# Weight-block sums of a Strassen-Winograd FFN made by adding transfers instead of GpSimd instructions

## What is computed

```python
def _swiglu(h, w_gu, w_down):
    g, u = jnp.split(h @ w_gu, 2, axis=-1)
    return (jax.nn.silu(g) * u) @ w_down
# in each layer:
h = h + _swiglu(_rmsnorm(h, norm_ffn[i]), ffn_w_gu[i], ffn_w_down[i])
```

## Time and profile before

| | |
|---|---|
| timed runs | 1211.78, 1214.74, 1216.09 us (median 1214.74) |
| profiled execution | 1215.77 us, span 1213.9 us, mean granted clock 0.988 |
| PE busy | 1133.1 us (93%) |
| DVE busy | 863.2 us (71%) |
| POOL busy | 672.8 us (55%) |
| ACT busy | 537.8 us (44%) |
| DMA | 98.32 MB, mean 81 GB/s; 97.16 MB of it through SyncE's queue, none from GpSimd's |

### The profile page before, as it was taken

How to read it: one execution, slowest core, us unless ns; L and a number is a source line. 1 busy time by engine, 2 the same in 40 slices (tenths; PEclk the granted TensorE clock), 3 DMA queues, 4 the chain that set the end, 5 groups by cost and what they waited for, 6 DMA issues and landing times.

```text
span 1213.9 us, 18428 instructions
## 1 busy us (share of the span) xinstructions
PE 1133.1 (93%) x7114; PEld 1011.2 (83%) x7114; DVE 863.2 (71%) x1260; ACT 537.8 (44%) x1053; POOL 672.8 (55%) x583
## 2 busy tenths in 40 slices
PE   9999998899899998999999999997989899988897
PEld 8877676888788988978998888876988788988786
DVE  6688776688744889845398888675898435889643
ACT  6487634454301545411277777433544103445202
POOL 6477654777424676534255545645776225776442
PEclk9999998999999999999999999998999999999999
DMA  6311133223333332332211001141323332332331
GB/s 189 99 35 53 36 109 82 70 71 104 96 96 88 87 105 70 107 95 93 80 38 38 18 19 35 53 142 49 105 73 91 96 106 77 98 103 72 96 96 70
DMA packets 175397, 98.32 MB, mean 81 GB/s; under 512 B 7880, under 2 KB 171216, under 8 KB 175312
## 3 DMA queue, kind: packets, MB, share of 16 engines
q1 hardware_dynamic: 175296, 97.16, 28.1%
q10 hardware_dynamic: 16, 0.00, 0.0%
HBM read 94.01 MB, written 2.10 MB: 79 GB/s over the span
## 4 chain that ended last, share of the span: by engine, by line
PE 51%; DVE 30%; ACT 7%; issue 7%; POOL 4%; DMA 1%; DVEq 0%; ACTq 0%; POOLq 0%
PE bank L1640 13%; PE bank L1644 13%; PE bank L1643 13%; DVE w_lo L2937 7%; DVE gate_up L2969 5%; DVE f_lo L2974 3%; DVE gate_up L2953 3%; DVE gate_up L2958 3%; ACT w_hi L1292 3%; PE bank L2346 2%; ACT f_hi L1317 2%; DVE gate_up L2954 2%; DVE g_lo L2937 1%; PE bank L2365 1%; PE bank L2368 1%
## 5 line engine op out<-in xcount | busy, mean ns | idle before, releaser
L1640 PE MATMUL bank<-x_hi,w_lo 128*128 128x256 f32 (+1 forms) x424 | 136.8, 323 | 21.4 <-DVE w_lo L2937 12.6
L1640 PE MATMUL bank<-f_hi,w_lo 128*128 128x512 f32 (+1 forms) x363 | 141.6, 390 | 13.5 <-DVE f_lo L2974 13.5
L1643 PE MATMUL bank<-f_lo,w_hi 128*128 128x512 f32 (+1 forms) x363 | 140.3, 387 | 0.0
L1644 PE MATMUL bank<-f_hi,w_hi 128*128 128x512 f32 (+1 forms) x363 | 140.2, 386 | 0.0
L1643 PE MATMUL bank<-x_lo,w_hi 128*128 128x256 f32 (+1 forms) x424 | 134.9, 318 | 0.0
L1644 PE MATMUL bank<-x_hi,w_hi 128*128 128x256 f32 (+1 forms) x424 | 134.8, 318 | 0.0
L835 POOL TENSOR_TENSOR s<-raw 128x512 f32<-128x512 f32 x40 | 64.1, 1601 | 104.0 <-DVE g_lo L2937 74.0
L822 POOL TENSOR_SCALAR w_hi<-raw 128x1408 fp32r<-128x1408 f32 x32 | 44.0, 1376 | 127.6 <-PE bank L1644 116.3
L853 POOL TENSOR_TENSOR gate_s<-gate_s,rs_t 128x512 f32<-128x512 f32 x44 | 65.9, 1497 | 81.5 <-ACT gate_s L1309 81.5
L2937 DVE TENSOR_TENSOR w_lo<-raw,w_hi 128x1024 fp32r<-128x1024 f32 x80 | 93.8, 1173 | 22.7 <-ACT w_hi L1292 22.7
L1640 PEld LDWEIGHTS bank<-x_hi,w_lo 128*128 128x128 f32 x424 | 83.8, 198 | 28.5 <-issue 14.2
(11 more groups left out here) (372 smaller groups left out, 3849.8 us busy)
## 6 DMA issues: line engine op xcount, KB each, us to landing
raw<-in_ffn_w_gu SPq DMA_DIRECT2D x80, 512.0 KB, 5.2
raw<-in_ffn_w_down SPq DMA_DIRECT2D x32, 704.0 KB, 4.6
w_raw<-in_a_w_qkv SPq DMA_DIRECT2D x10, 512.0 KB, 4.7
w_raw<-in_a_w_o SPq DMA_DIRECT2D x8, 512.0 KB, 4.0
w_raw<-in_ffn_w_gu SPq DMA_DIRECT2D x8, 512.0 KB, 3.9
w_raw<-in_b_w_o SPq DMA_DIRECT2D x8, 512.0 KB, 3.8
w_raw<-in_b_w_in SPq DMA_DIRECT2D x4, 672.0 KB, 4.0
w_raw<-in_b_w_uq SPq DMA_DIRECT2D x4, 576.0 KB, 3.9
```

Of the source, the lines that this page charges most:

```text
L1640: first = pe.matmul(o, ll, rh, start=start, stop=False)
L1643: pe.matmul(o, lh, rl, start=False, stop=False)
L1644: return pe.matmul(o, lh, rh, start=False, stop=stop)
```

## The change

GpSimd no longer adds. ScalarE writes the negated a21 and a22 into one of two buffers s_pair (new `minus`, one activation of 128 x 1024). From GpSimd's queue four transfers are issued that add their source into their destination: a21 += a22 in the raw slot (s1); -a21 += a11 (s3); -a22 += s3 (s2, with the other sign); and s_last += that (s4), where SyncE has loaded a12 into s_last anew (`seed`). The groups are now: group 0 a11 and a12, group 1 s1 and a22, group 3 s3 and s2, group 2 s4. The two differences on the activations' side change their signs to match (L2902, L2904). The seven products use the groups in the order 0, 0, 1, 1, 3, 2, 3, and the lists of ScalarE, VectorE and GpSimd are rewritten.

```diff
         (s43,) = region(scratch + 48 * 1024, [("s43", [P, 2 * QUART], F32)])
-        g1_hi, g1_lo = region(w_start, [("g1_hi", [P, 2 * QUART], F32R), ("g1_lo", [P, 2 * QUART], F32R)])
+        s_pair = (s43, s12)
+        g1_hi, g1_lo, s_last = region(w_start, [
+            ("g1_hi", [P, 2 * QUART], F32R), ("g1_lo", [P, 2 * QUART], F32R), ("s_last", [P, QUART], F32)])
         raw_slot = (raw_0, raw_1)
 
...
-        def group_raw(r, g):
+        def group_raw(u, r, g):
 
             raw = raw_slot[r % 2]
-            return (raw[:, 0:2 * QUART], s12[:], raw[:, 3 * QUART:4 * QUART],
-                    s43[:].rearrange("p (w k n) -> p k w n", w=2, k=HK))[g]
+            return (raw[:, 0:2 * QUART], raw[:, 2 * QUART:4 * QUART], s_last[:],
+                    s_pair[u % 2][:].rearrange("p (w k n) -> p k w n", w=2, k=HK))[g]
+
+        GROUPS_DONE = (1, 2, 4, 3)
...
-                        sp.wait_ge(g_ready, 4 * unit_of(past // RAW_LAYER, j) + 4)
+                        sp.wait_ge(g_ready, 4 * unit_of(past // RAW_LAYER, j) + 2)
+                        sp.wait_ge(s3_in, 16 * (unit_of(past // RAW_LAYER, j) + 1))
                     else:
                         half, m = (0, at - UNITS_0) if at < UNITS_0 + KD else (1, at - FFN_UNITS - KD)
...
+                def seed(j):
+                    u = unit_of(layer, j)
+                    if j == 2:
+                        sp.wait_ge(w_ready, c0 + 4)
+                    if u:
+                        sp.wait_ge(g_ready, 4 * u)
+                    dst = s_last[:].rearrange("p (k n) -> p k n", n=P)
+                    sp.dma_start(dst, gu_v[layer][:, HK:KD, j, :]).then_inc(seed_in, 16)
 
                 load(c0 // 2, 0, gu_v[layer][:, :, 0, :], P)
                 load(c0 // 2, 1, gu_v[layer][:, :, FB, :], P)
...
-            def sums_12(layer, j):
+            def sums(layer, j):
 
                 u, r = unit_of(layer, j), raw_unit(layer, j)
-                raw = raw_slot[r % 2]
-                a11, a21, a22 = (raw[:, i * QUART:(i + 1) * QUART] for i in (0, 2, 3))
-                pool.wait_ge(raw_in[r % 2], raw_landed(r))
-                if u:
-                    pool.wait_ge(g_ready, 4 * (u - 1) + 2)
-                if j == 2:
-                    pool.wait_ge(t_ready, 4 * layer + HK)
-                pool.tensor_tensor(s12[:, 0:QUART], a21, a22, ALU.add).then_inc(s12_ready, 1)
...
-            def sums_43(layer, j):
-
-                u, r = unit_of(layer, j), raw_unit(layer, j)
-                raw = raw_slot[r % 2]
-                a11, a12, a21 = (raw[:, i * QUART:(i + 1) * QUART] for i in (0, 1, 2))
-                if u:
-                    pool.wait_ge(g_ready, 4 * (u - 1) + 4)
-                pool.tensor_tensor(s43[:, QUART:2 * QUART], a11, a21, ALU.subtract).then_inc(s43_ready, 1)
-                pool.wait_ge(s12_ready, 2 * u + 2)
-                pool.tensor_tensor(s43[:, 0:QUART], a12, s12[:, QUART:2 * QUART], ALU.subtract).then_inc(s43_ready, 1)
+                a11, a21, a22 = (raw_slot[r % 2][:, i * QUART:(i + 1) * QUART] for i in (0, 2, 3))
+                s3, s2 = (s_pair[u % 2][:, i * QUART:(i + 1) * QUART] for i in range(2))
+                pool.wait_ge(minus_ready, u + 1)
+                pool.dma_start(a21, a22, accum_op=ALU.add).then_inc(s1_in, 16)
+                pool.dma_start(s3, a11, accum_op=ALU.add).then_inc(s3_in, 16)
+
+            def more_sums(layer, j):
+
+                u = unit_of(layer, j)
+                s3, s2 = (s_pair[u % 2][:, i * QUART:(i + 1) * QUART] for i in range(2))
+                pool.wait_ge(s3_in, 16 * (u + 1))
+                pool.dma_start(s2, s3, accum_op=ALU.add).then_inc(s2_in, 16)
+                pool.wait_ge(s2_in, 16 * (u + 1))
+                pool.wait_ge(seed_in, 16 * (u + 1))
+                pool.dma_start(s_last[:], s2, accum_op=ALU.add).then_inc(s4_in, 16)
 
...
                 for j in range(j0 if half else 2, j1):
-                    if j > j0 and j > 2:
+                    if j > j0:
                         scale_gate(layer, j - 1)
                     if j + 1 < j1:
-                        sums_43(layer, j + 1)
+                        sums(layer, j + 1)
+                        more_sums(layer, j + 1)
                     else:
                         down_hi(layer, c0, half, 0)
                         down_hi(layer, c0, half, 1)
-                    if j + 2 < j1:
-                        sums_12(layer, j + 2)
...
+            def minus(layer, j):
+
+                u, r = unit_of(layer, j), raw_unit(layer, j)
+                act.wait_ge(raw_in[r % 2], raw_landed(r))
+                if j == 2:
+                    act.wait_ge(ss_ready, norms[2 * layer + 1].base + KD)
+                elif j == 3:
+                    act.wait_ge(t_ready, 4 * layer + HK)
+                else:
+                    act.wait_ge(g_ready, 4 * (u - 2) + 3)
+                act.activation(s_pair[u % 2][:], raw_slot[r % 2][:, 2 * QUART:4 * QUART], ACT.Copy, scale=-1.0) \
+                    .then_inc(minus_ready, 1)
+
             def group_hi(layer, j, g):
 
                 c0, u, r = (C_FFN0, C_FFN1)[layer], unit_of(layer, j), raw_unit(layer, j)
-                if g in (0, 2):
+                if g == 0:
                     act.wait_ge(raw_in[r % 2], raw_landed(r))
                 elif g == 1:
-                    act.wait_ge(s12_ready, 2 * u + 2)
+                    act.wait_ge(s1_in, 16 * (u + 1))
+                elif g == 2:
+                    act.wait_ge(s4_in, 16 * (u + 1))
                 else:
-                    act.wait_ge(s43_ready, 2 * u + 2)
+                    act.wait_ge(s2_in, 16 * (u + 1))
...
-                    act.wait_ge(m_done, 7 * (u - 1) + (2, 4, 5, 7)[g])
-                act.activation(G_HI[g], group_raw(r, g), ACT.Copy).then_inc(g_hi_ready, 1)
+                    act.wait_ge(m_done, 7 * (u - 1) + (2, 4, 6, 7)[g])
+                act.activation(G_HI[g], group_raw(u, r, g), ACT.Copy).then_inc(g_hi_ready, 1)
...
-                act.wait_ge(m_done, 7 * u + (1, 3, 4, 7)[which])
+                act.wait_ge(m_done, 7 * u + (1, 3, 5, 7)[which])
...
                 for j in range(j0 if half else 2, j1):
                     if j > 2 and j > j0:
                         take_product(layer, j - 1, 3)
                     group_hi(layer, j, 3)
+                    group_hi(layer, j, 2)
                     take_product(layer, j, 0)
                     if j > 2 and j > j0:
                         silu(layer, j - 1)
                     if j + 1 < j1:
+                        minus(layer, j + 1)
                         group_hi(layer, j + 1, 0)
+                    if j > j0:
+                        f_high(layer, j - 1)
                     take_product(layer, j, 1)
                     take_product(layer, j, 2)
-                    if j > j0:
-                        f_high(layer, j - 1)
                     if j + 1 < j1:
                         group_hi(layer, j + 1, 1)
-                        group_hi(layer, j + 1, 2)
...
                     pe.wait_ge(t_ready, 4 * layer + HK)
                 pe.wait_ge(g_ready, 4 * u + 2)
                 one(side[:, 0:HT], 1, 0, ts(0))
+                one(apart[:, HT:T], 1, 1, ts(3))
+                pe.wait_ge(g_ready, 4 * u + 3)
                 pe.wait_ge(m_read, 4 * u + 1)
-                one(main[:, 0:HT], 1, 1, ts(1), start=False)
-                pe.wait_ge(g_ready, 4 * u + 3)
-                one(apart[:, HT:T], 2, 0, ts(3))
+                one(main[:, 0:HT], 3, 1, ts(1), start=False)
                 pe.wait_ge(g_ready, 4 * u + 4)
                 pe.wait_ge(m_read, 4 * u + 2)
-                one(side[:, 0:HT], 3, 0, xs(HK, late), start=False)
+                one(side[:, 0:HT], 2, 0, xs(HK, late), start=False)
                 pe.wait_ge(m_read, 4 * u + 3)
-                one(main[:, 0:HT], 3, 1, ts(2), start=False)
+                one(main[:, 0:HT], 3, 0, ts(2), start=False)
...
-                dve.wait_ge(g_hi_ready, 4 * u + g + 1)
-                dve.tensor_tensor(G_LO[g], group_raw(r, g), f(G_HI[g]), ALU.subtract).then_inc(g_ready, 1)
+                dve.wait_ge(g_hi_ready, 4 * u + GROUPS_DONE[g])
+                dve.tensor_tensor(G_LO[g], group_raw(u, r, g), f(G_HI[g]), ALU.subtract).then_inc(g_ready, 1)
...
                 for j in range(j0 if half else 2, j1):
                     if j > 2 and j > j0:
                         rest_of_unit(layer, j - 1)
                     group_lo(layer, j, 3)
+                    group_lo(layer, j, 2)
+                    if j > j0:
+                        hidden(layer, j - 1)
                     if j + 1 < j1:
                         group_lo(layer, j + 1, 0)
                     else:
                         down_lo(layer, c0, half, 0)
                     if j > j0:
-                        hidden(layer, j - 1)
                         f_low(layer, j - 1)
+                    late_gate(layer, j)
                     if j + 1 < j1:
```

(49 more changed lines are left out.)

13 lines of the change are left out of this document (2 added, 11 removed).

## The result

The changed kernel takes 1420.72 us (median of 4 runs, 1415.93 to 1424.95), the kernel before 1215.3 us beside it. The ratio is 1.1696, 95% interval [1.1649, 1.1742]: slower by 205 us, where 1298 us were forecast and the range ended at 1395. The direction was right, the size was not.

The account below looks back on a forecast made before the run. VectorE, slowed by GpSimd's sums, often bound the kernel before; afterwards a loop of 3.0 + y per unit would. Stages 140.4 + 36y = 540.0 us, 90.5 more, less 8: net 82.5 on 1215.8, so 1298 us; range 1180 to 1395.

Parts of the forecast that it names:

- The bound of before: Product stages before the change: GpSimd's sums make VectorE late and TensorE waits; faster helpers could give back 46 us.
- The loop (3.0 + y): Once per unit through ScalarE and GpSimd, from one landing of s4 to the next: 14.1 us instead of 11.65.
- fixed steps: ScalarE's group 2, product copy and gate activation, then GpSimd's scaling of the gate: together 3.0 us per unit.
- link: One adding transfer, from its issue to the next issue or, for s4, its landing; forecast from a 3.1 us row.
- The term y: Per unit: issue of s1 0.6, three serial adding transfers at 3.1 each, 1.2 for sharing with raw loads: 11.1 us.
- the sum: All four product stages together: 140.4 + 36y = 540.0 us, 90.5 more than the 449.5 before.
- The ends of a stage: First late s4 lands 3.5 + y behind a stage's start; 7.6 us stand behind the last s4.
- What was outside the stages: At each layer's first stage TensorE's 4.30 us idle shrinks: 4 us back per layer, 8 in all.
- The rival of the copy's price: Adding transfers land like copies, 2.4 us each: y 7.8, 1180 us; chance 0.20, including up to break-even.
- The rival of the slow transfers: Adding transfers are as slow as loads, 4.7 us each: y 14.7, 1428 us; chance 0.13 for y over 12.5.
- TensorE's clock: Matmuls behind long gaps run at half speed for some microseconds; counted as nothing, TensorE having 4 us spare per unit.

Follow-up runs that it names:

- the fastest version: Changed kernel with s3 and s2 as GpSimd instructions and, on ScalarE's list, group 2 later and the second product copy ahead of the hidden block's high part: 1178.52 us.

## Why the prediction was wrong in size

- **The bound of before.** Borne out: VectorE, slowed by GpSimd's additions. Its hidden product fell from 1775 to 807 ns in the changed kernel, and the fastest version lost 47 us when its two transfers were made additions again.
- **The loop (3.0 + y).** Right in every step and its order. Its fixed steps measured 2.74 us instead of 3.0 (1.51 on ScalarE, 1.23 on GpSimd). Taking one link out saved 4.2 us for each y, taking the landing of s4 out saved 106 us.
- **The term y, forecast 11.1 us.** This is the step that failed: the price of the three adding transfers one behind another, which I took at 3.1 us each, from the row of a 512 KB store ("the row it is nearest to"), with 0.6 us on two of them for the raw loads. Over the 32 rounds y measured 14.5 us (0.6 for the issue of s1, links of 4.9 and 4.7, landing of 4.2). That is 3.4 us too little, 36 times: 122 of the 135 us by which the stages (675.1 us) exceed the forecast (540.0). With the raw loads small the three took 5.1, 3.9 and 3.3 us in the mean, 12.3 in all instead of 9.3. The largest part is s3: it runs behind s1, and in the last rounds beside the loads of the down blocks, and the sum had both at nothing. The landing alone, 3.3 us in quiet, was 0.2 us too low, and the 0.3 us from a landing to GpSimd's next issue was left out twice. And the raw loads cost 1.6 us a round by the rows, 1.8 by the time, not 1.2. The price of a plain copy, the rival's 2.4 us, was right for the landing; adding costs 3.4 us per y on top of it.
- **The ends of a stage.** Here the sum was short by 5 us in each of the four stages. From the last scaling behind a landed s4 to the first down matmul it had 6.1 us; the trace has 8.5 to 9.0. TensorE's clock is in this, which I had put at nothing. Products 6 and 7 stand on the path there, and behind a wait of 5.8 us the clock was at its lower level (start us, us, operation; then length, busy, clock):

```profile
358.02 0.55 PE L2107 MATMUL bank<-t_hi,x_lo 128*128 128x256 f32 x1 [5.76 <-ACT m_u L1327]
```

```profile
362.00:366.50 4.50, 3.78 (x18) 3.81 (x19) 2.20 (x3) 0.85 (x3) 0.73 (x1) 0.50 0.43 124
```

  The matmuls then start 0.21 us apart instead of 0.12. At the start of a stage the first late s4 lands 19.7 to 20.9 us in, where the sum gives 18.0 with the measured y; what makes that is open. Against both stand the fixed steps, 8 us too dear in all.
- **What was outside the stages.** I counted 8 us back at the layers' starts. 25.5 us came back. The first stage begins at 214.63 instead of 220.49, its wait of 4.30 us gone, and the second layer's gains about as much. The rest, which I had not seen, stands behind the stages: before the change TensorE waited there for VectorE's last low part of the hidden block (3.4, 2.9, 4.1 and 3.0 us in the four stretches), and after it 0.2, 0.7, 0.2 and 0.5 us.
- **The rival of the copy's price.** It gave 1180 us for copies that land in 2.4 us. Of the three transfers in the loop two did so in the median, s4's copy took 4.5 us beside the raw load, and the time was 1299 us. With the loads made small all three did, and it was 1229 us: the rounds beside the first and the down loads, which the sum has at the same price, took 15 to 17 us instead of 11.
- **The rival of the slow transfers.** Its price of 4.7 us per transfer stood 7 us from the result, and the three links measured 4.6 us in the mean. Its reason, that an adding transfer is as slow as a load, is not what the runs show: it lands in 3.3 us with nothing beside it, and the longer landings stand where other transfers run beside it. That the price was met is in part luck. I gave y over 12.5 a chance of 0.13.
- **TensorE's clock.** The stages ran at 0.83, and I had counted nothing. The loop does not contain TensorE's work, so within the rounds the clock costs nothing that the rows show, and what one link less saved agrees with the link alone. It enters at the ends of the stages, as above. No run holds the clock up, so its share is not shown apart.

## What to carry to other kernels

When work moves to transfers that feed each other, write down the loop that they close, on all engines' lists, before anything else: a wait placed ahead of unrelated work closes it, and one instruction's place was worth 106 us here. Price a link from its issue to the next issue, with neighbours on the same engines, not by a landing time from a quiet stretch. Give to transfers only those sums that no one on the issuing engine waits for: two of four, with ScalarE's list put in order, made 3%, where all four cost 17%.

## What the hardware showed that I had not expected

- An adding transfer of 256 KB took 1.64 us of all 16 engines, a copy 0.74 us, and its packets were 144 instead of 80 (23040 and 12800 over 160). It landed in 3.3 us with nothing beside it, the copy in 2.3 to 2.4.
- Its issue kept GpSimd 0.85 us, and 1.17 us where it came right behind another; a copy's kept it 0.54 to 0.58 us in either place. This time lay inside the transfer's own landing time: 0.3 us behind a landing the next issue started.
- VectorE's 128x512 step with two SBUF operands took 0.69 us alone and 1.77 us beside a GpSimd addition. With three GpSimd instructions in a unit instead of five, the units fell from 12.4 to 10.9 us.
